# The stores of the feed-forward's first phase issued from GpSimd's queue instead of SP's

## What is computed

```
for l in range(DEPTH):
    mod = (cond @ w_ada[l] + b_ada[l])[:, None, :]
    shift_a, scale_a, gate_a, shift_f, scale_f, gate_f = jnp.split(mod, N_MOD, axis=-1)
    h = rms_norm(x) * (1.0 + scale_a) + shift_a
    x = x + gate_a * hybrid_mixer(h, ...)
    h = rms_norm(x) * (1.0 + scale_f) + shift_f
    x = x + gate_f * (jnp.square(jax.nn.relu(h @ w_mlp_up[l])) @ w_mlp_down[l])
```

## Time and profile before

| | |
|---|---|
| median of 3 runs | 3516.66 us (3513.88 to 3517.92) |
| the profiled execution | 3516.78 us, span 3515.5 us |
| mean granted clock of TensorE | 0.981 |
| busy: PE, DVE, ACT, POOL | 96%, 57%, 37%, 13% of the span |
| first phase of the feed-forward | layer 0 from about 650 to 967 us, layer 1 to 2197 us |
| stores to hidden | 224, from 659.9 to 2198.8 us, all in SP's queue |
| DMA through SP's queue (q1) | 398.56 MB, 32.4% of the 16 engines' span |
| DMA through GpSimd's queue (q0) | 123.28 MB, 10.6% |

### The profile page before, as it was taken

How to read it: one execution, slowest core, us unless ns; L and a number is a source line. 1 busy time by engine, 2 the same in 40 slices (tenths; PEclk the granted TensorE clock), 3 DMA queues, 4 the chain that set the end, 5 groups by cost and what they waited for, 6 DMA issues and landing times. The chain is left out here.

```text
span 3515.5 us, 42813 instructions
## 1 busy us (share of the span) xinstructions
PE 3379.8 (96%) x16731; PEld 2293.9 (65%) x16731; DVE 2009.8 (57%) x3578; ACT 1286.0 (37%) x2245; POOL 472.6 (13%) x575
## 2 busy tenths in 40 slices
PE   7999899899999989998999999999999997999998
PEld 4666567688888866665677887888775683333333
DVE  3666684877757656666848666576664743000002
ACT  2444333455544334443335555443330621111111
POOL 1222110000000002221100000000110002444443
PEclk9999999999999999999999999999999998999999
DMA  6000362355575560003722444754600317887633
GB/s 233 28 28 22 125 248 92 120 177 174 190 257 192 192 223 28 28 22 110 254 91 102 153 154 167 254 193 171 202 15 1 127 61 273 283 307 250 216 96 120
DMA packets 270228, 525.22 MB, mean 149 GB/s; under 512 B 46192, under 2 KB 117560, under 8 KB 263884
## 3 DMA queue, kind: packets, MB, share of 16 engines
q1 hardware_dynamic: 238652, 398.56, 32.4%
q0 software_dynamic: 29920, 123.28, 10.6%
q10 hardware_dynamic: 1456, 0.66, 0.1%
HBM read 615.18 MB, written 114.82 MB: 208 GB/s over the span
## 5 line engine op out<-in xcount | busy, mean ns | idle before, releaser
L226 PE MATMUL psum<-arena_r,arena_r 128*128 128x512 f32 (+1 forms) x5084 | 1213.8, 391 | 24.4 <-ACT arena_r L2179 10.5
L226 PEld LDWEIGHTS psum<-arena_r,arena_r 128*128 128x128 f32 x5084 | 960.0, 190 | 227.3 <-issue 12.5
L226 PE MATMUL psum<-arena 128*128 128x128 f32 (+8 forms) x3834 | 764.8, 376 | 18.5 <-ACT arena L1043 7.6
L226 PEld LDWEIGHTS psum<-arena 128*128 128x128 f32 (+1 forms) x3834 | 468.6, 192 | 270.8 <-issue 193.3
L4373 PE MATMUL psum<-arena 128*64 128x512 f32 x1536 | 341.2, 596 | 6.1 <-DMA arena<-in_expert_w_gate,be_i 5.3
L2312 ACT ACTIVATE arena_r<-arena 128x1024 fp32r<-128x1024 f32 x192 | 192.2, 1051 | 327.4 <-PE psum L226 302.0
L2473 DVE TENSOR_TENSOR arena_r<-arena,arena_r 128x1024 fp32r<-128x1024 f32 x192 | 225.8, 1220 | 135.9 <-ACT arena_r L2312 135.8
L269 POOL TENSOR_SCALAR stat<-stat 128x1 f32<-128x1 f32 (+1 forms) x120 | 36.3, 303 | 1985.4 <-ACT arena L1018 665.4
L4505 DVE TENSOR_TENSOR arena<-arena,psum 128x512 f32<-128x512 f32 x24 | 16.5, 687 | 427.3 <-PE psum L4373 427.3
L234 PEld LDWEIGHTS psum<-const,arena 128*128 128x128 f32 (+1 forms) x1439 | 169.0, 153 | 132.6 <-issue 82.5
L4373 PEld LDWEIGHTS psum<-arena 128*64 128x64 f32 x1536 | 108.8, 137 | 214.7 <-issue 211.0
(11 more groups left out here) (469 smaller groups left out, 3971.8 us busy)
## 6 DMA issues: line engine op xcount, KB each, us to landing
tmp_hidden<-arena SPq DMA_DIRECT2D x224, 256.0 KB, 2.0
arena<-tmp_hidden SPq DMA_DIRECT2D x112, 512.0 KB, 4.8
arena<-in_w_mlp_down SPq DMA_DIRECT2D x96, 512.0 KB, 6.3
arena<-in_w_ada SPq DMA_DIRECT2D x36, 1024.0 KB, 7.7
weight_ring<-in_w_mlp_up SPq DMA_DIRECT2D x32, 1024.0 KB, 5.5
tmp_x_res<-arena SPq DMA_DIRECT2D x32, 512.0 KB, 5.8
arena<-in_w_in SPq DMA_DIRECT2D x6, 2048.0 KB, 14.4
arena<-tmp_x_res SPq DMA_DIRECT2D x24, 512.0 KB, 8.4
```

Of the source, the lines that this page charges most:

```text
L226: i = self.nc.tensor.matmul(out, lhs, rhs, start=start and n == 0, stop=stop and n == len(pairs) - 1, skip_group_check=read_between)
```

## The change

`sp_hidden` and `sp_up_late` become `pool_hidden` and `pool_up_late` and use GpSimd's queue. `pool_up_chunks` holds the waits and stores of the phase in the order in which they stood in SP's sequence, and `pool_ff` calls it in both layers. `sp_up_chunks` keeps the loads: conditioning weights, up weights, and turns 0 and 1 of the second phase. No other engine's sequence changes, and no semaphore's value.

```
--- before.py
+++ after.py
@@ -2012,46 +2012,48 @@
     k.nc.sync.dma_start(k.ff.wide[up_slot(n)], wu[:, :, at(n, 256)]).then_inc(*ff_arrived(k, up_slot(n)).dma("up", l, n))
 
 
-def sp_hidden(k, l, kind, n):
-
-    k.nc.sync.dma_start(k.d["hidden"][n, KINDS.index(kind)], hidden_place(k, kind, n)).then_inc(*hidden_stored(k, kind).dma(l, n))
-
-
-def sp_up_late(k, l, n):
-
-    S_, E = k.S, k.sp
+def pool_hidden(k, l, kind, n):
+
+    k.nc.gpsimd.dma_start(k.d["hidden"][n, KINDS.index(kind)], hidden_place(k, kind, n)).then_inc(*hidden_stored(k, kind).dma(l, n))
+
+
+def pool_up_late(k, l, n):
+
+    S_, E = k.S, k.pool
     E.wait_ge(S_.up_act.at("u21", l, n))
-    sp_hidden(k, l, "21", n)
+    pool_hidden(k, l, "21", n)
     E.wait_ge(S_.up_dve.at("s4", l, n))
-    sp_hidden(k, l, "s4", n)
+    pool_hidden(k, l, "s4", n)
+
+
+def pool_up_chunks(k, l):
+    S_, E = k.S, k.pool
+    for n in range(FFC):
+        if n > 0:
+            pool_up_late(k, l, n - 1)
+        E.wait_ge(S_.up_act.at("u11", l, n))
+        pool_hidden(k, l, "11", n)
+        E.wait_ge(S_.up_dve.at("s3", l, n))
+        pool_hidden(k, l, "s3", n)
+        E.wait_ge(S_.up_act.at("u22", l, n))
+        pool_hidden(k, l, "22", n)
+        E.wait_ge(S_.up_dve.at("s1", l, n))
+        pool_hidden(k, l, "s1", n)
+        E.wait_ge(S_.up_dve.at("s2", l, n))
+        pool_hidden(k, l, "s2", n)
+    pool_up_late(k, l, FFC - 1)
 
 
 def sp_up_chunks(k, l):
     S_, E = k.S, k.sp
     for n in range(FFC):
-        if n > 0:
-            sp_up_late(k, l, n - 1)
-        if l + 1 < DEPTH and n == 0:
-            sp_ada_unit(k, l + 1, 0)
-        E.wait_ge(S_.up_act.at("u11", l, n))
-        sp_hidden(k, l, "11", n)
+        if l + 1 < DEPTH:
+            sp_ada_unit(k, l + 1, n)
         if n + 2 < FFC:
             E.wait_ge(S_.up_dve.at("low", l, n, 4), S_.up_act.at("high", l, n, 4))
             sp_up(k, l, n + 2)
-        if l + 1 < DEPTH and n + 1 < FFC:
-            sp_ada_unit(k, l + 1, n + 1)
-        if n == FFC - 1:
-            sp_down(k, l, 0)
-            sp_down(k, l, 1)
-        E.wait_ge(S_.up_dve.at("s3", l, n))
-        sp_hidden(k, l, "s3", n)
-        E.wait_ge(S_.up_act.at("u22", l, n))
-        sp_hidden(k, l, "22", n)
-        E.wait_ge(S_.up_dve.at("s1", l, n))
-        sp_hidden(k, l, "s1", n)
-        E.wait_ge(S_.up_dve.at("s2", l, n))
-        sp_hidden(k, l, "s2", n)
-    sp_up_late(k, l, FFC - 1)
+    sp_down(k, l, 0)
+    sp_down(k, l, 1)
 
 
 def down_arrived(k, part, q):
@@ -2316,6 +2318,7 @@
     if l + 1 < DEPTH:
         before_ff(k, k.pool, l)
         k.nc.gpsimd.memset(k.ada_unit.bias, 0.0).then_inc(*k.S.ada_pool.up("unit_zero", l + 1))
+    pool_up_chunks(k, l)
 
 
 def dve_up_sum(k, l, n, p):
```

## The result

| | before | after |
|---|---|---|
| median, same chip | 3516.49 us (3513.88 to 3522.61, 6 runs) | 3534.77 us (3531.97 to 3541.18, 6 runs) |
| ratio to before | | 1.0053, 95% interval 1.0042 to 1.0063 |
| profiled execution | 3516.78 us, span 3515.5 | 3541.18 us, span 3539.9 |
| mean granted clock | 0.981 | 0.977 |

The change costs 18.3 us. That lies outside the predicted range (3514.0 to 3529.0), on the side of "slower".

The account below looks back on a forecast made before the run. TensorE, without idle time in both first phases, was taken to bound the kernel. The last s4's late landing stalls it 1.8 us in each layer: 3516.8 + 3.6 = 3520.4 us, with clock at 0; range 3514.0 to 3529.0.

Parts of the forecast that it names:

- The middle of the phase is free: First phase, chunks 0 to 14: their stores on GpSimd cost nothing, hidden by the chunk's 19.2 us.
- The slack of 0.1 and 0.5 us: Turn 1 of the second phase: VectorE's low parts end 0.1 (layer 0) and 0.5 us (layer 1) before TensorE needs them.
- The reason given for the wait, shared memory: Turn 1: ScalarE's second high part waits for s4's store because its output overwrites s4's place.
- 0.84 us from start to start: Last four stores on GpSimd: 0.54 us issue plus 0.30 us gap between each; high end 1.29 us.
- The chain behind the landing: Before turn 1: from s4's landing to the last low part takes 4.6 us in both layers.
- the first of the change: SP loses 224 issues: loads of turns 0 and 2 go out earlier, not worth time; removal costed at nothing.
- Landing: Last s4 before turn 1: lands 5.1 us after issue (ends 1.9 and 6.3), stalling TensorE 1.8 us a layer.
- Clock: After the stall at turn 1: granted clock costs 0; high end 2 x 1.7 = 3.4 us.
- B: Turn 1: GpSimd's queue of four stores is slow and the clock falls, 9.8 us, 3526.6 us; chance 0.20.
- A: Turn 1: s4 lands 3.8 and 2.9 us after issue, as from SP; 0.5 us stall in layer 1, 3517.3; chance 0.25.
- C: Inside chunks: GpSimd's issues hold VectorE up, 32 chunks x 0.54 = 17 us, 3534 us; chance 0.05.
- D: End of first phase: earlier loads remove waits of 1.62 and 0.57 us, at most 4.4 us faster, 3512.4; chance 0.05.

Follow-up runs that it names:

- last_chunk_sp: Changed kernel, but the last chunk's seven stores are back on SP in their old order, 210 stores staying on GpSimd: 3519.01 us, ratio 1.0000.
- after_no_wait: Changed kernel without ScalarE's wait for the landing of s4 before turn 1's second high part: 3520.46 us, ratio 1.0005.
- hold_turn2: Changed kernel, all stores on GpSimd, but SP's loads of turn 2 wait until s4 has landed: 3521.77 us, ratio 1.0010.
- half_turn2: Changed kernel, with two of turn 2's four loads (1 MB) held until s4 has landed: 3532.64 us, ratio 1.0040.
- turn2_first: Kernel before, all stores on SP, but turn 2's loads put ahead of the last four stores: 3533.88 us, ratio 1.0045.
- last_four_pool: Kernel before, with only the last chunk's s1, s2, u21 and s4 on GpSimd; turn 2's loads move up: 3532.27 us, ratio 1.0038.
- s4_from_act: Changed kernel, but the last s4 alone is started by ScalarE, directly ahead of its own wait: 3530.88 us, ratio 1.0037.
- before_no_wait: Kernel before without ScalarE's wait for the landing of s4 at turn 1: 3517.87 us, ratio 0.9995.

## Why the prediction was wrong

**Right.** The middle of the phase is free: last_chunk_sp gives 1.0000. The one path to TensorE at the end of the phase is ScalarE's wait for the last s4, and without that wait (after_no_wait) the stall is gone. The slack of 0.1 and 0.5 us is borne out: measured from the start of turn 0, ScalarE went on 4.6 and 5.9 us later than before, and the stalls were 4.38 and 5.25. The reason given for the wait, shared memory, is wrong, as shown above. GpSimd starts s4 at 970.2, and the trace has 970.3, 0.6 us of which is the shift of the trace. The working behind it was off: I took 0.84 us from start to start by way of the indirect DMAs' gap, and direct stores stand 0.53 us apart; s4 went out 0.5 us sooner than forecast. The chain behind the landing took the 4.6 us: 978.59 + 4.6 = 983.2, turn 1 began at 983.32.

**The step that failed** is the first of the change: "Neither is worth time. ... I cost the removal at nothing." I asked what the earlier loads could gain and found nothing, which holds. I didn't ask what they could take. One premise beside it is false as well: "Turn 2's places come free only when turn 0 is over". That is so for the high parts that ScalarE writes. The places of the loads themselves were free earlier: in after the first went out at 967.34, before turn 0 began at 967.79. The loads of turn 2 aren't awaited by anybody, and they moved from behind the only store that somebody awaits to in front of it. The prediction even names it ("turn 2's loads, 2 MB, now go out at about 2196, before s4 instead of after it"), but prices it with another stage's 5.1 us, where 64 KB stores pass beside loads. That row is no measure of a 256 KB store behind three others and 2 MB issued within 3 us. The two sized terms that followed from it:

- *Landing*: forecast 5.1, high end 6.3, measured 8.2 and 9.1 us. Stall forecast 1.8 + 1.8, measured 4.38 + 5.25 = 9.6 us, above the high end of 8.8. hold_turn2 gives the same GpSimd stores without the loads: s4 landed after 2.9 and 3.0 us, so the order of the transfers is worth 5.3 and 6.1 us of the landing.
- *Clock*: forecast 0, high end 3.4, measured 2.2 + 1.6 = 3.8 us. A stall of 1.6 us left the clock alone. Every stall before turn 1 in these traces, from 2.71 to 5.95 us, was followed by matmuls at 0.50. The shortest two are those of half_turn2, 3.35 us in layer 0 and 2.71 in layer 1:

```profile
984.00:988.00 4.00, 3.82 (x9) 3.08 (x10) 4.00 (x5) 2.18 (x3) 0.00 (x0) 0.50 0.97 361
```

```profile
2222.00:2226.00 4.00, 3.50 (x9) 2.81 (x10) 4.00 (x5) 2.50 (x3) 0.00 (x0) 0.57 1.01 376
```

Both are stretches of half_turn2, in the columns of the earlier trace rows. The 0.57 is a mean of both levels: from 2222.5 to 2225.5 the clock was 0.50. How long it stays low doesn't go by the length of the stall: after 5.54 us (turn2_first, layer 1) the same stretch, 2222 to 2226, also had 0.57.

**The rivals.** B had the right shape, stall plus clock, 3526.6 us, at too low a landing, and for the wrong reason: GpSimd's own spacing. A is refuted; its landing "as it was" appears only when the loads are held back. The 0.4 us later first byte of the Trainium skill ("DMA: Bandwidth & Descriptors", Latency and other measured facts) is small beside the order. No run here shows a first byte by itself. From issue to landing, GpSimd's stores in the middle of layer 0's phase took 2.6 us by the median where SP's took 2.0; at the end of the phase, held back, GpSimd's last stores landed in 2.8 to 2.9 us, and SP's s4 had taken 2.9. C's number, 3534 us, is almost the result, and C is false: in after the list of TensorE's waits names none from 700 to 950 us, and last_chunk_sp, with 210 of the 224 issues that C charges for, costs nothing. A total that fits is no evidence for a mechanism. D is refuted: the waits of 1.62 and 0.57 us stand in after as 1.62 and 0.53.

The rule of the Trainium skill, "SBUF — State Buffer" (SBUF: two separate sides), that I weighed under C would have made stores go out late in the phase. The 86 mid-phase issues of after took 539 to 548 ns each, so no issue was held. Whether a part of the 0.6 us by which they landed later than SP's comes from it isn't shown.

**What stays open.** The stretches account for 14.2 us and turn2_first for 15 (its interval reaches from 11 to 21), against 18.3 (15 to 22). The intervals overlap, so a second cause isn't shown; after_no_wait and hold_turn2 leave 1.5 and 2.8 us that could be one.

The traces of before and after can be laid side by side, as both have the same 16731 matmuls in the same order. The profiled pair differs by 24.4 us: 0.6 us before layer 0's turn 0, 6.9 in its second phase, 6.1 from there to layer 1's turn 0, 7.3 in layer 1's second phase, and 3.4 after it. Of the 6.1, 5.3 arise between 1600 and 1800 us, in layer 1's attention, and most of these are clock: from 1640.5 to 1647.0 us after was granted 0.50, and the same matmuls in before (1632 to 1636.5) had 0.91. That need not come from the moved stores. In last_four_pool, with eight stores on GpSimd, the same place costs 3.0 us; in s4_from_act, with all but two of the 224 on GpSimd, and in last_chunk_sp, with 210, it costs nothing. And before_no_wait, with all stores on SP, loses 2.7 us against before between 2460 and 2600 us. There is one trace of each kernel, so it isn't known how far such stretches come and go from run to run.

GpSimd itself has one gap in that attention in which it waited for nothing that the profile shows. It is the list of GpSimd's waits of after, 1600 to 1700 us, and then of last_chunk_sp:

```profile
POOL tmp_mixed L1400 <- issue: 5.9, 1, 5.9
```

```profile
POOL tmp_mixed L1400 <- issue: 4.1, 1, 4.1
```

after_no_wait, hold_turn2 and half_turn2 have it too (5.8 to 6.2 us), s4_from_act doesn't. In the four kernels where it is 5.8 us or more, TensorE waits 0.4 to 0.7 us for ScalarE (L1522) in the same attention, a wait that before and last_chunk_sp don't have. By that wait the gap is worth under 1 us; its cause stays open.

## What to carry to other kernels

When an edit takes work out of a queue, list what stood behind it: these transfers now start sooner, and a big load that nobody awaits yet can get ahead of a small store that somebody does. A second queue doesn't protect the store, as the DMA engines are shared; an explicit hold of the load does. And of every wait for a landing, ask which memory it protects: here the stall came through a wait that protected none, and went with it.

## What the runs showed of the hardware

- A 256 KB store issued behind 2 MB of loads landed after 8.2 and 9.1 us (GpSimd), 8.4 and 7.9 us (ScalarE's queue) and up to 8.9 us (SP), and after 2.9 and 3.0 us without these loads ahead. With 1 MB ahead it was 7.2 and 6.6 us.
- A store's landing is 16 updates of its semaphore. They came within 1.1 us in after and over 3.0 us in half_turn2 (s4, layer 0), and the last one counts.
- Direct stores of 128 rows on GpSimd are started 0.53 us apart, three in a row, without the 0.30 us gap that stood between indirect ones.
- TensorE's stall of 1.62 us before the last pass cost no clock. All stalls before turn 1, from 2.71 to 5.95 us, were followed by matmuls at a granted clock of 0.50, the level of 1.2 GHz. In after this was worth 2.2 and 1.6 us on top of the stalls.
